# Attention layer: ScalarE's split of the next weight slot moves behind two copies

## The reference, cut to what matters

```
q, k, v, gate = split(x @ in_w, 4)                 # 8 heads, two maps of 64 each, v of 128
# prompt, by blocks of 128 queries
s = q @ k.T * 64**-0.5, causal;  p = softmax(s)
w = p[map 0] - lam * p[map 1];   o = w @ v
# samples: 1024 past positions in pages of a cache (8 pages of 128 rows a sample), then the 4 new ones
p = softmax(concat(q @ k_past.T, q @ k.T));  w = p[map 0] - lam * p[map 1]
o = w @ concat(v_past, v)
y = (rms_norm(o) * silu(gate)) @ out_w
```

## Time and profile before

| | |
|---|---|
| Median of 3 runs | 1734.4 us (1726.73 to 1735.77) |
| Profiled execution | 1729.82 us, span 1728.1 us |
| Mean granted TensorE clock | 0.932 of full speed |
| TensorE busy, matmuls | 1506.2 us (87%) |
| TensorE busy, weight loads | 1351.6 us (78%) |
| VectorE busy | 1017.5 us (59%) |
| ScalarE busy | 717.2 us (42%) |
| GpSimd busy | 593.5 us (34%) |
| The layer's span | about 297 to 768 us |

### The profile page before, as it was taken

How to read it: one execution, slowest core, us unless ns; L and a number is a source line. 1 busy time by engine, 2 the same in 40 slices (tenths; PEclk the granted TensorE clock), 3 DMA queues, 4 the chain that set the end, 5 groups by cost and what they waited for, 6 DMA issues and landing times. The chain is left out here.

```text
span 1728.1 us, 33603 instructions
## 1 busy us (share of the span) xinstructions
PE 1506.2 (87%) x12742; PEld 1351.6 (78%) x12742; DVE 1017.5 (59%) x2157; ACT 717.2 (42%) x1331; POOL 593.5 (34%) x681
## 2 busy tenths in 40 slices
PE   5998968999898897859589999999998799699894
PEld 5887958777777775649489999999997699488793
DVE  4788351445545555462545779777976531668834
ACT  1666142343443434321424455454545311466613
POOL 1544413212221210125223354535545445054440
PEclk6999989999999998979779999999998899799997
DMA  3222205566657566522013144324343133022211
GB/s 118 68 66 77 81 15 157 173 197 186 199 156 216 164 184 193 176 74 74 4 50 86 53 114 110 102 55 124 101 111 101 41 84 86 15 76 67 76 54 52
DMA packets 282249, 178.68 MB, mean 103 GB/s; under 512 B 18874, under 2 KB 280794, under 8 KB 282088
## 3 DMA queue, kind: packets, MB, share of 16 engines
q1 hardware_dynamic: 282088, 176.53, 35.1%
HBM read 159.62 MB, written 16.86 MB: 102 GB/s over the span
## 5 line engine op out<-in xcount | busy, mean ns | idle before, releaser
L171 POOL TENSOR_TENSOR w_low<-w_raw,w_high 128x256 fp32r<-128x256 f32 x608 | 529.3, 900 | 1031.5 <-ACT w_high L162 983.5
L162 ACT ACTIVATE w_high<-w_raw 128x1024 fp32r<-128x1024 f32 x152 | 160.2, 1054 | 223.9 <-PE proj_lo L195 83.4
L1587 PE MATMUL proj<-xh,w_high 128*128 128x288 f32 x440 | 137.6, 313 | 2.7 <-POOL w_low L171 2.7
L1587 PE MATMUL proj<-xl,w_high 128*128 128x288 f32 x440 | 132.1, 300 | 0.0
L1587 PE MATMUL proj<-xh,w_low 128*128 128x288 f32 x440 | 131.9, 300 | 0.0
L1587 PE MATMUL proj_lo<-xh,w_high 128*128 128x256 f32 x440 | 128.3, 292 | 2.0 <-ACT u L1836 2.0
L1587 PE MATMUL proj_lo<-xl,w_high 128*128 128x256 f32 x440 | 125.4, 285 | 0.0
L1587 PE MATMUL proj_lo<-xh,w_low 128*128 128x256 f32 x440 | 124.7, 283 | 0.0
L1587 PEld LDWEIGHTS proj_lo<-xh,w_high 128*128 128x128 f32 x440 | 84.3, 192 | 11.2 <-issue 8.9
L1587 PEld LDWEIGHTS proj<-xh,w_high 128*128 128x128 f32 x440 | 85.5, 194 | 5.0 <-POOL w_low L171 3.2
L1587 PEld LDWEIGHTS proj<-xh,w_low 128*128 128x128 f32 x440 | 85.2, 194 | 0.0
(11 more groups left out here) (432 smaller groups left out, 4418.2 us busy)
## 6 DMA issues: line engine op xcount, KB each, us to landing
k_pages<-in_cache_k SPq DMA_DIRECT2D x256, 128.0 KB, 2.5
v_pages<-in_cache_v SPq DMA_DIRECT2D x256, 128.0 KB, 2.3
w_raw<-in_c_in_w SPq DMA_DIRECT2D x48, 512.0 KB, 4.0
w_raw<-in_a_in_w SPq DMA_DIRECT2D x32, 512.0 KB, 4.0
w_raw<-in_b_in_w SPq DMA_DIRECT2D x32, 512.0 KB, 4.5
w_raw<-in_a_out_w SPq DMA_DIRECT2D x16, 512.0 KB, 4.2
st<-in_state_ssd_h SPq DMA_DIRECT2D x16, 512.0 KB, 5.5
out_ssd_h_sample<-st SPq DMA_DIRECT2D x16, 512.0 KB, 5.4
```

The source lines that it names most:

```text
L162: act.activation(k.wh[par][:], k.raw[par][:], ACT.Copy).then_inc(k.sem["w_hi"], 1)
L171: step = pool.tensor_tensor(k.wl[par][:, tiles, :], k.raw[par][:, tiles, :], k.wh[par][:, tiles, :], ALU.subtract)
L1587: mm = pe.matmul(out, w[par][:, i, :], x[:, i, cols], start=first and opens and i == 0 and n == 0, stop=last and i == KT - 1 and n == 2, s ...
```

## The change

In `b_scalar`, the block that splits the next slot moves from before the copy of key quarter 2 to behind the copy of the prompt's weights. Nothing else changes; in periods without a slot the order is the same as before.

```diff
         if p.scored:
             duo_softmax(*p.scored)
-        if p.slot:
-            at = s0 + p.slot + 1
-            split_high(act, k, at, at // 2, at % 2)
         if p.unit:
             for q in KEYS_ACT:
                 if q >= 2:
                     keys_copy(act, k, *p.unit, q, copy)
         if p.before:
             weights_copy(*p.before)
+        if p.slot:
+            at = s0 + p.slot + 1
+            split_high(act, k, at, at // 2, at % 2)
         if p.unit:
             prompt_softmax(*p.unit)
```

## The result

| | before | after |
|---|---|---|
| Median of 7 runs | 1734.4 us (1726.73 to 1738.58) | 1718.31 us (1713.62 to 1724.31) |
| Ratio to before, 95% interval | | 0.9925 (0.9904 to 0.9947) |
| Profiled execution | 1729.82 us, span 1728.1 | 1719.59 us, span 1717.9 |
| Mean granted TensorE clock | 0.932 | 0.935 |
| From the layer's first key transposes to its last mean of squares | 464.6 us | 449.9 us |

The kernel is 0.75% faster, by 0.53 to 0.96%: the ratio is estimated from all the runs, and the plain quotient of the two medians, 0.9907, lies inside its interval. The forecast was 1721; the profiled execution, forecast at 1719.2 by its own measure, took 1719.6. That second agreement is partly luck, as the last two lines of the table show: the layer gained 14.7 us, four more than the sum said, and the rest of the program gave 4.7 back.

The account below looks back on a forecast made before the run. TensorE's own order of work was taken to bound the kernel. Eleven waits shortened by 0.96 us gave -10.6 us, all else nothing; from the 1731.7 us mean of four executions this made 1721, range 1712 to 1731.

Parts of the forecast that it names:

- the sum: All parts of the change added up: -10.6 us, from 11 shortened TensorE waits, every other part taken as nothing.
- The bound and the wait: Attention layer, 297 to 640 us: TensorE's order sets the pace; 11 L896 waits for ScalarE's key copy total 16.6 us.
- The 0.96 us: Even periods: quarter 2's copy starts 0.96 us earlier, cutting TensorE's wait from 1.51 to 0.55 us, 11 times.
- No other condition takes over: Weights' transposes, even periods: VectorE's weights and the keys are ready early enough, so the whole 0.96 us is gained.
- Odd periods, cost nothing: ScalarE, odd periods: it idles 2.39 us before quarter 2's copy, so going first gains nothing; the later split is covered.
- GpSimd's margin of 2.5 us: Tightest period, at 412 us: the later low part still ends 2.5 us before TensorE's next high half; cost nothing.
- SP's queue: SP's load of the slot after next stands 2.8 us awaiting the low part; cost nothing, DMA share up 3%.
- The split delays the prompt's softmax: ScalarE: the split fits idle time before the softmax, narrowest 1.03 us; cost nothing, at most 0.1 us a period.
- Collisions: VectorE beside GpSimd's moved low part, odd periods with a normalisation: cost nothing to 5.3 us, taken as nothing.
- case B: Rival, chance 0.12: the gain is made, but normalisations colliding with the low part lose 5.3 us, giving 1726 us.
- Case C: Rival, chance 0.14: less idle time avoids two TensorE lower-clock stretches at 465 and 585 us, 3.2 us more, giving 1718.
- A: The forecast itself, chance 0.66: the attention layer's shorter waits give 1721 us.

Follow-up runs that it names:

- the quarters exchanged: Kernel before, split left in place, VectorE copying key quarter 2 and ScalarE quarter 3: 1718.08 us, ratio 0.9936.
- the late split: Changed kernel with the split moved further, behind the prompt's softmax: 1731.12 us, ratio 1.0015 to the kernel before.
- GpSimd held back: Changed kernel, GpSimd waiting in even periods for the prompt's maxima before the low part: 1713.27 us (0.9889), timed again 1719.88 us (0.9938).

## Why the prediction came out right

- *The bound and the wait.* Right. TensorE's order sets the pace, and the 11 waits at L896 for the copy of quarter 2 were what the move shortened. Four other edits that free that bank in time (behind quarter 2 only, in even periods only, earlier, the quarters exchanged) give stretches of 449.4 to 450.0 us, the change itself 449.9 to 451.3. The slotted stretch is 12.3 us shorter, where 10.6 was forecast: 3.0 more by the two drops, 1.2 less by L945.
- *The 0.96 us.* Right: waits of 0.56 to 0.58 us where 0.55 was worked out, 10.3 us over the 11 where the sum had 10.6. That the next instruction starts 0.96 us behind the split's start, and not 1.06, held.
- *No other condition takes over.* Right in all periods, the one with four key blocks included (0.58 us).
- *Odd periods, cost nothing.* Right; moving them changes nothing.
- *GpSimd's margin of 2.5 us, and SP's queue.* Right: TensorE waits nowhere for a low part in the slotted stretch, and in the tightest period the low part ends at 413.70 us and the next high half starts at 416.19. SP waits more:

```profile
SPq L155 <- POOL w_low L171: 18.0, 11, 3.4
```

  from 297 to 640 us, against 4.2 us in three waits before. Nobody waits for SP; the longest, 3.4 us, is near the 2.8 us that was worked out.
- *The split delays the prompt's softmax.* Right, and as narrow as it was called ("by less than 0.1 us"). In the tight period no idle time is left:

```profile
409.76 1.05 ACT L162 ACTIVATE w_high<-w_raw 128x1024 fp32r<-128x1024 f32 x1
410.83 0.37 ACT L1103 ACTIVATE p_prompt<-s,p_max 128x128 f32<-128x128 f32 x1
```

  VectorE's maximum (L1243) ends at 410.79 there, so the softmax starts on time, with nothing to spare. The 1.58 us left in the period at 378 us are no measure of the margin: that period is roomier, and 0.39 us of them are the lateness of the maximum.
- *Collisions.* The step that failed, though the total did not hang on it. It looked for the place where a low part would reach a long VectorE instruction, and found the reciprocal at L1265, at nothing to 5.3 us. The low part does lie elsewhere: it meets L1243 and L1211, which I had not considered because they are 0.17 and 0.15 us long. What counts is not an instruction's length but what it releases: the maximum releases ScalarE's softmax and everything behind it. The place was wrong and the price 1.2 us, inside the bounds. The sentence that no row shows a reciprocal beside a low part missed one. The trace of before has one, behind the layer's last period:

```profile
764.04 3.75 DVE L1265 RECIPROCAL rms<-rms 128x576 f32<-128x576 f32 x1 [3.19 <-ACT rms L1118]
767.83 7.60 DVE L1272 SCALAR_TENSOR_TENSOR o_feat<-o_feat,subln,rms 128x512 f32<-128x512 f32 x1
```

```profile
765.03 2.81 POOL L171 TENSOR_TENSOR w_low<-w_raw,w_high 128x256 fp32r<-128x256 f32 x4 [52.13 <-ACT w_high L162]
767.79 7.08 POOL L843 TENSOR_TENSOR xT<-xh,xl 128x3264 f32<-128x3264 f32 x1
```

  The reciprocal has its usual 3.75 us with a low part beside it, so case B as I placed it could have been excluded. The row after it shows the other side: an instruction of 0.75 us takes 7.60 beside one long GpSimd instruction.
- *The clock.* Case C, with 0.14, came true beside A: two drops gone, 3.0 us, forecast at 3.2. I had argued that the link to the wait was not certain, since the same wait at 412 us had no drop; in the second profile of before it has one. Not each such wait brings a drop, but 11 of them brought two or three in each profile, and none of the ten profiles in which those 11 were short had one. So the chance was too low. Had C been taken whole, the forecast would have been 1718, which is what the median shows. I don't count the 0.3 us between them as a success, since the spread of the runs is over 10 us.
- *The basis.* I started from 1731.7, the mean of four executions, not from their median of 1734.4. The kernel before, timed beside the experiments, had medians of 1729.55, 1730.68 and 1730.55, so the lower basis was the nearer one there; beside the result it was 1734.4. That 1721 is only 2.7 us above the measured median is in part luck of this choice: the drops gave 3 us and more that the sum did not have, and the low basis took 2.7 off beforehand. From the median the forecast would have been 1723.8. As a ratio the sum's 10.6 us are 0.9939, inside the measured 0.9904 to 0.9947.

## What to carry to other kernels

When an engine in order has a long filler instruction between a buffer's being full and the copy that empties it, the producer waits longer by the filler's length, and this can be read off two timelines; move the filler to where the engine idles, or give the copy to another engine, and count the gain as the start-to-start time times the periods. Then follow the filler's consumer: every instruction that it will newly lie beside has to be looked up, the tiny ones first if they release a chain; and look even where the filler stays, since the rest of the period moves. And a recurring wait of the matmul engine can be worth more than its own length: here two or three stretches at the lower clock went with eleven waits of 1.5 us. Count that as a chance and not as certain, since two waits of the same length elsewhere brought none.

## What the runs showed of the hardware

- A VectorE instruction of 128x2 elements beside a GpSimd instruction takes 0.56 instead of 0.17 us, and one of 128x1 0.69 instead of 0.15, while a reciprocal of 128x576 stays at 3.75. The wait fits the end of one GpSimd piece: the low part from 379.54 us on is four pieces in 2.84 us, so by equal pieces (an estimate) they end at 380.25, 380.96, 381.67 and 382.38, and the two VectorE instructions end at 381.01 and 381.69. Beside one piece of 7.08 us the loss is 6.85 us (7.60 against 0.75).
  The Trainium skill ("SBUF — State Buffer", Who interferes with whom) says that a VectorE operation which needs the shared ports and a GpSimd operation exclude each other for the whole length of the one that holds them. The losses here agree: 0.39 and 0.54 us beside pieces of about 0.7, and 6.85 beside one of 7.08.
- That last loss stands before the output projection, for which TensorE waits 8.85 and 10.31 us in the first profiles of the two kernels (9.30 and 10.30 in the other two of before, 8.79 and 8.77 in those of after, so the difference is not the kernels'). Cutting L843 into pieces, or placing it later, was not tried; it is the next thing I would try, and its gain is open.
- TensorE's clock: stretches at the lower level (mean 0.51 over 3.3 us in the earlier trace rows) cost 1.5 us each. In the slotted part all ten of them, seven before the change and three in the late split, followed waits of 1.5 to 2.1 us; two waits of 1.53 or 1.54 us at L931 in each of the ten faster profiles brought none. In the state-space layer, where TensorE is hardly ever idle (10.00 of 10 us busy in the row at 1074 us), single drops come 58 us apart in some executions of either kernel and not in others. Their cause stays open. The tail varies by up to 12 us between profiles; the drops are a part of that, but not all of it: with GpSimd held back the two tails are 957.6 and 951.4 us at the same mean clock of 0.93.
